# First projections in quarters of the features, small loads moved, and a buffer of its own for the third projection's weights

## The reference, cut to what matters

```
mod = silu(c) @ w_ada + b_ada             # 6 x 1024 columns; c_ctx for the context tile
sh1, sc1, g1, sh2, sc2, g2 = split(mod, 6)
h = layer_norm(x) * (1 + sc1) + sh1
q_a, k_a, v_a, q_g, k_g, v_g, r_g, lr, mg = split(h @ w_in)
attn = attention(rms(q_a), rms(k_a), v_a)        # rotary on latents, cached keys and values
gla  = gated linear attention(q_g, k_g, v_g, decay from lr)  # chunks of 64, both directions
merged = sigmoid(mg0) * (attn @ w_br_attn) + sigmoid(mg1) * (gla * silu(r_g) @ w_br_gla)
x  = layer_norm(alpha * x + g1 * (merged @ w_out))
h2 = layer_norm(x) * (1 + sc2) + sh2
x  = layer_norm(alpha * x + g2 * mixture_of_experts(h2))     # 32 experts, top 1 of 4 groups, top 2 of 8
```

## Time and profile before

| | |
|---|---|
| three executions, us | 663.35, 665.12, 667.0 (median 665.12) |
| the profiled execution, us | 667.03, span 665.3 |
| PE busy | 619.1 us, 93% of the span, 3423 matmul instructions |
| DVE, ACT, POOL busy | 266.9, 107.2, 114.5 us |
| DMA | 176.5 MB, 265 GB/s in the mean |
| longest links of the chain that ended last | PE 70%, DMA 15%, DVE 8% of the span |

### The profile page before, as it was taken

The page is one execution under the profiler, slowest core; times in us unless marked ns, Lnnn a source line. Parts: engine busy times, 40 slices in busy tenths (PEclk is TensorE's granted clock), DMA queues, the critical chain, the costliest instruction groups (busy, mean ns, idle before and its releaser), DMA issues.

```text
span 665.3 us, 8643 instructions
## 1 busy us (share of the span) xinstructions
PE 619.1 (93%) x3423; PEld 348.1 (52%) x3423; DVE 266.9 (40%) x600; ACT 107.2 (16%) x223; POOL 114.5 (17%) x113
## 2 busy tenths in 40 slices
PE   6998999999999999999999999999999987778894
PEld 3553345546455556565554575665565543444541
DVE  4321543135534543302325866334333333222247
ACT  2001543211022322240000012111111111111000
POOL 4000000110300000000001222434334333221101
PEclk9999999999999999999999999999999999999898
DMA  9997737345030330308995089999999999999952
GB/s 340 391 330 282 253 128 254 127 132 186 24 128 9 118 109 19 96 32 244 398 404 249 32 320 355 349 418 415 412 417 417 414 415 413 416 417 418 411 226 95
DMA packets 56120, 176.50 MB, mean 265 GB/s; under 512 B 10378, under 2 KB 12458, under 8 KB 44432
## 3 DMA queue, kind: packets, MB, share of 16 engines
q1 hardware_dynamic: 39264, 143.34, 55.5%
q10 hardware_dynamic: 11152, 24.47, 10.5%
q0 software_dynamic: 5664, 8.14, 3.5%
HBM read 174.32 MB, written 11.96 MB: 280 GB/s over the span
## 4 chain that ended last, share of the span: by engine, by line
PE 70%; DMA 15%; DVE 8%; issue 3%; ACT 2%; POOL 1%; SPq 0%; ACTq 0%; DVEq 0%; POOLq 0%
PE bank L1619 13%; PE bank L1901 12%; PE bank L1608 7%; PE bank L1793 6%; PE bank L1910 5%; DMA Y<-exp_w_up 4%; PE bank L1807 4%; DMA X<-exp_w_up 4%; DMA W<-exp_w_up 4%; PE bank L1572 3%; PE bank L1532 2%; DMA Y<-w_ada 2%; PE bank L1875 2%; POOL rstd L706 1%; PE bank L1760 1%
## 5 line engine op out<-in xcount | busy, mean ns | idle before, releaser
L1901 PE MATMUL bank<-X,Y 128*64 128x256 f32 x672 | 80.6, 389 | 12.4 <-DMA X<-exp_w_up 11.4
L1619 PE MATMUL bank<-Y,W 128*128 128x384 f32 x256 | 86.6, 492 | 0.0
L1901 PEld LDWEIGHTS bank<-X,Y 128*64 128x64 f32 x672 | 51.0, 135 | 46.8 <-DMA X<-exp_w_up 18.4
L706 POOL TENSOR_TENSOR rstd<-ss,cst 128x1 f32<-128x1 f32 (+3 forms) x21 | 22.6, 1074 | 294.4 <-DVE ss L839 294.4
L1619 PEld LDWEIGHTS bank<-Y,W 128*128 128x128 f32 x256 | 47.4, 190 | 36.0 <-issue 5.6
L1608 PE MATMUL bank<-W,Y 128*128 128x512 f32 x144 | 64.0, 598 | 0.0
L749 POOL DMA_INDIRECT Y<-h_rows,gidx x31 | 40.3, 1301 | 86.0 <-PE bank L1875 80.5
L1218 DVE COPY abias<-bank 128x128 f32<-128x128 f32 x32 | 9.3, 292 | 111.5 <-PE bank L1937 111.5
L1901 PE MATMUL bank<-W,Y 128*64 128x256 f32 (+1 forms) x320 | 37.7, 340 | 7.1 <-DMA W<-exp_w_up 3.4
L754 POOL DMA_INDIRECT pair_rows<-PTr,sidx x32 | 32.9, 1029 | 64.6 <-DVE PTr L1232 64.0
L1608 PEld LDWEIGHTS bank<-W,Y 128*128 128x128 f32 x144 | 26.7, 190 | 30.9 <-issue 30.6
(11 more groups left out here) (237 smaller groups left out, 731.5 us busy)
## 6 DMA issues: line engine op xcount, KB each, us to landing
X<-exp_w_gate SPq DMA_DIRECT2D x22, 1024.0 KB, 25.5
X<-exp_w_up SPq DMA_DIRECT2D x22, 1024.0 KB, 26.3
X<-exp_w_down SPq DMA_DIRECT2D x22, 1024.0 KB
Y<-w_ada ACTq DMA_DIRECT2D x16, 1024.0 KB, 8.3
W<-w_in SPq DMA_DIRECT2D x7, 2048.0 KB, 9.2
W<-exp_w_gate SPq DMA_DIRECT2D x10, 1024.0 KB
W<-exp_w_up SPq DMA_DIRECT2D x5, 1024.0 KB
W<-exp_w_down SPq DMA_DIRECT2D x5, 1024.0 KB
```

The source lines that it names most:

```text
L706: nc.gpsimd.tensor_tensor(rstd[:, 0:n], ss[:, 0:n], const("mhalf", 0, n), ALU.pow)\
L1619: ins = mm(bank[:, 0:TOKENS], w[:, k, c * P:(c + 1) * P], hT[:, :, k, :], start=k == 0, stop=k == KT - 1)
L1901: ins = mm(bank[hh * 64:hh * 64 + 64, a:b], x_[:, c, h * 64:h * 64 + 64], rhs(hh), start=k == 0 and a == 0, stop=k == KT - 1, skip_group_c ...
```

## The change

- `w_ada`'s first 2048 columns and the first two projections' weights are loaded in four quarters: quarter g holds columns 256g to 256g+255 of the shift and of the scale (1 MB each) and feature blocks 2g and 2g+1 of `kvl` and `gqk`. PE's `shift_scale(g)` multiplies a quarter of both at once (16 matmuls of 256 columns where `modulation` had 8 of 512), `columns(g)`, `modulate(g)` and `project_quarter(kind, i, g)` follow by quarters.
- Only `ident` and `selcol` are loaded first; the other constants after the second quarter. The small parameters come ahead of the fourth quarter; the router's weights come last, with a semaphore of their own.
- `vg`'s weights go to three pieces of memory that are free until later (`vg_parts`), so their load waits only for `shift_scale(0)`; `q`, `rg` and the rest use the two halves of `W`.
- DVE takes the statistics of tiles 0 and 1 ahead of the silu, and has a slot for each tile's mean and power. The constant -1/2 is set by POOL.
- `keep_busy` is 4 at the start, 1 after the first `columns`; its moving operand is the identity, repeated.
- `ada` entries stand at 3, 6, 7, 8, 9, 10, 11, 13, `rows` 0 at 9 in place of 8. ACT issues eight bias rows in place of four at the start, and the three halves of the ring after `shift_scale(3)`.

The core of the diff:

```diff
-for _n, _j in zip(range(4, 12), (2, 4, 6, 7, 8, 10, 11, 13)):
+for _n, _j in zip(range(4, 12), (3, 6, 7, 8, 9, 10, 11, 13)):
     AFTER[_j].insert(0, ("ada", _n))
-AFTER[8].insert(0, ("rows", 0))
+AFTER[9].insert(0, ("rows", 0))
...
-FILL_START = 6
+FILL_START = 4
+FILL_QUARTER = 1
...
+QUARTERED = ("kvl", "gqk")
+QUARTERS = 4
+QK = KT // QUARTERS
+QD = QK * P
...
+        vg_parts = [(qT.rearrange("p i k t -> p (i k t)"), 0, 3), (Pr.rearrange("p b n -> p (b n)"), 3, 6),
+                    (q.rearrange("p i n -> p (i n)"), 6, 8)]
...
-            sp.dma_start(cst[:, :], T["consts"][:, 0:NCONST]).then_inc(S["consts_in"], 16)
+            early_consts = CAT["incl_f"]
+            sp.dma_start(cst[:, 0:early_consts], T["consts"][:, 0:early_consts]).then_inc(S["first_consts_in"], 16)
...
+            def load_shift_scale(g):
+                h = slice(QD * (g % 2), QD * (g % 2 + 1))
+                for n in (g // 2, 2 + g // 2):
+                    sp.dma_start(early[n][:, g % 2], wa[:, :, n * HALF + h.start:n * HALF + h.stop])\
+                        .then_inc(shift_scale_in[g], 16)
...
+            for g in range(QUARTERS):
+                load_shift_scale(g)
+                load_quarter(g)
+                if g == 1:
+                    sp.dma_start(cst[:, early_consts:], T["consts"][:, early_consts:NCONST]).then_inc(S["consts_in"], 16)
+                if g == 2:
+                    small_loads()
+            main.wait_full(sp, "shift_scale", 0)
+            for a, k0, k1 in vg_parts:
+                sp.dma_start(a[:, 0:(k1 - k0) * HALF].rearrange("p (k n) -> p k n", n=HALF),
+                             wi[:, k0:k1, OFF[5]:OFF[5] + HALF]).then_inc(S["vg_in"], 16)
+            router_weights()
...
+            first_norm_stats(0)
+            first_norm_stats(1)
+            first_norm(0)
+            silu_of_cond()
+            first_norm_stats(2)
+            first_norm(1)
+            first_norm(2)
+            for g in range(QUARTERS):
+                shift_scale(g)
+                modulate(g)
...
-            for n in range(4):
-                bias_rows(n)
+            for g in range(QUARTERS):
+                quarter_bias_rows(g)
...
-            main.wait_full(act, "ada", 3)
+            main.wait_full(act, "shift_scale", QUARTERS - 1)
             for h in range(3):
                 ada_half(h)
...
+            def shift_scale(g):
+
+                pe.wait_ge(shift_scale_in[g], 32)
+                bank = main.claim(pe, "shift_scale", g)
+                for s in range(2):
+                    w = early[2 * s + g // 2][:, g % 2]
+                    for k in range(KT):
+                        j = k % 4
+                        ins = mm(bank[32 * j:32 * j + 32, s * QD:(s + 1) * QD], csil[:, k, :], w[:, k, :], start=k < 4,
+                                 stop=k >= 4, skip_group_check=True)
+                main.filled(ins, "shift_scale", g)
...
             keep_busy(FILL_START)
             x_transposes(0)
             x_transposes(1)
             pe.wait_ge(S["cond_silu"], 2)
-            modulation(0)
+            shift_scale(0)
             x_transposes(2)
...
+            columns(0)
+            keep_busy(FILL_QUARTER)
+            for g in range(QUARTERS - 1):
+                for i in range(TILES):
+                    project_quarter("kvl", i, g)
+                project_quarter("gqk", 0, g)
+                shift_scale(g + 1)
+                project_quarter("gqk", 1, g)
+                columns(g + 1)
+                project_quarter("gqk", 2, g)
```

More of the change, by code:

```diff
@@ L97, in constants @@
     put("unused", np.repeat(EMPTY + (rows // SLOT_ROWS)[:, None], 2 * NE, 1))
-    put("mhalf", np.full((P, 8), -0.5))
     c[:, NCONST:] = 2 * np.arange(TOKENS)[None] + (rows // SLOT_ROWS)[:, None]
     return c
-WEIGHTS = ([("ada", 0)]
-           + [(x, 0) for x in ("kvl", "gqk", "vg", "q", "rg")] + [("mg", n) for n in range(4)]
+WEIGHTS = ([(x, 0) for x in ("kvl", "gqk", "vg", "q", "rg")] + [("mg", n) for n in range(4)]
            + [("br", n) for n in range(2)])
@@ L199, in wait_read @@
         eng.wait_ge(self.at[job][2], self.at[job][3] + 1)
-HALVED = ("kvl", "gqk")
+QUARTERED = ("kvl", "gqk")
+QUARTERS = 4
+QK = KT // QUARTERS
+QD = QK * P
 def first_jobs():
-    jobs = {("modc", g): 7 for g in range(2)}
+    jobs = {("modc", g): 7 for g in range(QUARTERS)}
     jobs.update({("xT", 0, 0): 0, ("xT", 0, 1): 1, ("xT", 1, 0): 3, ("xT", 1, 1): 0, ("xT", 2, 0): 1, ("xT", 2, 1): 3})
-    jobs.update({("ada", n): 2 for n in (0, 2, 1, 3, 4)})
-    for kind, ring in zip(HALVED, ((4, 5, 6), (3, 0, 1))):
+    jobs.update({("shift_scale", g): 2 for g in range(QUARTERS)})
+    jobs[("ada", 4)] = 2
+    for kind, ring in zip(QUARTERED, ((4, 5, 6), (3, 0, 1))):
         jobs.update({("proj", kind, 0, i): ring[i] for i in range(TILES)})
@@ L239, in main_jobs @@
     for j, x in enumerate(PROJ):
-        jobs += [("proj",) + x for _ in range(x[0] not in HALVED)] + [step for step in AFTER[j] if step[0] == "ada" and step[1] > 4]
+        jobs += [("proj",) + x for _ in range(x[0] not in QUARTERED)] + [step for step in AFTER[j] if step[0] == "ada" and step[1] > 4]
     jobs += [("br", c, m) for c in range(KT) for m in range(2)]
@@ L593, in _ @@
+            router_weights()
+            for j, (kind, n) in enumerate(ring):
                 buf = W[:, j % 2, :]
@@ L631, in _ @@
             load_gate_up(sp, 1, 1, ew_in[1])
[L632 to L633 removed]
+            sp.wait_ge(w_free[(len(ring) - 1) % 2], (len(ring) + 1) // 2)
+            sp.wait_ge(w_free[len(ring) % 2], len(ring) // 2)
             load_gate_up(sp, 3, 3, ew_in[3])
@@ L843, in power @@
                 dve.wait_ge(S["pow_done"], powers[0])
-            def norm(src, dst):
-                for g in range(2):
-                    step(V.bn_stats(stats[:, g, :], src[:, g * HALF:(g + 1) * HALF]))
-                step(V.bn_aggr(mv[:, :], stats[:, 0:2, :].rearrange("p a b -> p (a b)")))
-                power(ss[:, 0:1], mv[:, 1:2], 1.0, EPS)
-                return V.tensor_scalar(dst, src, mv[:, 0:1], rstd[:, 0:1], ALU.subtract, ALU.mult)
             def half_stats(src, g):
@@ L1313, in _, with quarter_bias_rows @@
             act.wait_ge(S["zeros_set"], 5)
+            def quarter_bias_rows(g):
+                bias, landed = quarter_bias(g)
+                for s in range(2):
+                    act.dma_start(bias[0:2, s * QD:(s + 1) * QD],
+                                  T["b_ada"][0:1, s * D + g * QD:s * D + (g + 1) * QD].to_broadcast([2, QD]))\
+                        .then_inc(landed, 16)
             def bias_rows(n):
@@ L1534, in modulation, with shift_scale, columns @@
                 main.filled(ins, "ada", n)
[L1535 to L1545 removed]
+            def shift_scale(g):
+                pe.wait_ge(shift_scale_in[g], 32)
+                bank = main.claim(pe, "shift_scale", g)
+                for s in range(2):
+                    w = early[2 * s + g // 2][:, g % 2]
[4 more added lines that the diff above has]
+                main.filled(ins, "shift_scale", g)
+            def columns(g):
+                bank = side.claim(pe, "modc", g)
+                main.wait_read(pe, "shift_scale", g)
+                for s in range(2):
+                    for j in range(QK):
+                        at = 2 * (s * KT + QK * g + j)
+                        c = s * QD + j * P
+                        ins = mm(bank[:, at:at + 2], part[:, g, c:c + P], const("selcol"), start=True, stop=True)
+                side.filled(ins, "modc", g)
             def keep_busy(count):
                 for _ in range(count):
[L1550 removed]
+                    mm(banks[6][:, :], ident, ident.unsqueeze(1).to_broadcast([P, HALF // P, P]), start=True, stop=True)
             def x_transposes(i):
```

241 lines of the change are left out of this document (102 added, 139 removed).

## The result

The kernel after the change takes **667.65 us** (median of 20 runs, 664.68 to 669.86), the kernel before 665.48 us (median of 20 runs beside them, 662.54 to 667.26). The ratio is 1.0035, 95% interval 1.0023 to 1.0048: slower by 1.5 to 3.2 us. I had forecast 663.3, a gain of 1.8. The time lies in my range, but the kernel is slower where I had forecast a gain; on that side I had given rival C (PE's clock) 0.15 and rival B (a late `ada` 4) 0.15. Ratios and mean clocks leave out executions more than 1.5% above the fastest of their kernel, of which there is one here, of e8 (671.05 us).

A forecast was written before the change was run, and what follows sets the result against it. PE's work was taken to bound the kernel, with gains only ahead of 25.26 us; `cum` 0 3.7 sooner less one `ada` (1.9) still to come nets 1.8, so 665.12 - 1.8 = 663.3 us, range 659.5 to 668.0.

The forecast's parts named there:

- rival C: PE's clock falls to its lower level in gaps of 1.9 and 3.8 us, 3.1 us each: 666.4 or 669.5; chance 0.15.
- rival B: `ada` 4's second ring half, issued only after `shift_scale(3)`, lands up to 2.9 us late, delaying the chain: 666.2; chance 0.15.
- The end of `ada` 4: On PE, after the fourth `kvl` quarter and `gqk` of tile 0, `ada` 4 ends at S + 33.3 + 6.7 = 59.2.
- S: Start of PE's first projection: 19.2 us, bounds 18.0 to 20.5, with second transposes at 13.1 set by DVE's order.
- `shift_scale`'s price: One quarter's shift and scale on PE, 32 instructions of 256 columns for 16 of 512: 1.95 us.
- Rival D: `shift_scale` is bound by its instructions, 3.5 us instead of 1.95, four times: 6.2 more, 669.5; chance 0.08.
- The quarters: First stage on PE: 11.1 us a quarter (`kvl`, `gqk`, `shift_scale`, 0.85 more), 33.3 for three.
- The moved small loads cost nothing, covered by this lead: Some 14 issues on SP ahead of the fourth quarter, which still lands before 44 and is needed at 46: no cost.
- The chain to the second `z`: Behind `ada` 4, DVE's bias add and key norm 4.3, gate step 4.2, with hand-overs 8.7: second `z` at 67.9.
- rival A: PE does not stand in the key norm's chain, so 3.8 us are not lost: 659.5; chance 0.20.
- From there to `cum` 0: From the second `z` to `cum` 0 on PE 12.5 us as before, so `cum` 0 starts at 80.4.
- The 1.27 us wait "stays": PE's 1.27 us wait for `w_ada` at 96.13 remains, as ACT issues that half at the same point of the order.

The follow-up runs named there:

- e8: e7 with DVE's last subtraction of each gate step moved behind the next key norm; 663.07 us, ratio 0.9960 to the kernel before.
- e9: Kernel after plus two PE fills between the transposes of tiles 0 and 1 only; 667.30 us, ratio 1.0030 to the kernel before.
- e13: Kernel after plus fills between the transposes of tiles 0 and 1, between `ada` 4's halves and ahead of the second `z`; 665.35 us, ratio 1.0004.
- e2: Kernel after plus two fills between the transposes of tiles 0 and 1 and three ahead of the second `z`; 665.44 us, ratio 1.0011.
- e1: Kernel after run again with no edit, as base of the others; 667.75 us, ratio 1.0039 to the kernel before.
- e3: Kernel after with the first key norm put ahead of `ada` 4's bias add, on DVE alone; 666.97 us, ratio 1.0019 to the kernel before.
- e7: Kernel after with e9's fill, e5's load order, gate work started earlier in the table and side banks changed; 667.81 us, ratio 1.0038.
- e15: Repeat of the best version: e8 with one ring half issued a quarter earlier, after `shift_scale(2)`; 660.25 us, ratio 0.9917 to the kernel before.
- e14: e15 without the split of DVE's gate step; 667.50 us, ratio 1.0027 to the kernel before.
- e4: Kernel after with the three ring halves issued by ACT after `shift_scale` 1, 2 and 3 instead of all after 3; 674.63 us, ratio 1.0144.
- e5: Kernel after with the 14 small loads issued behind the fourth quarter instead of ahead of it; 667.02 us, ratio 1.0017 to the kernel before.
- e6: Kernel after with the edits of e2 and e5 together; 665.88 us, ratio 0.9998 to the kernel before.

## Why the prediction was wrong, point by point

Two terms of the sum failed. The end of `ada` 4, put at 59.2, came at 61.5 to 61.9, and with it the second `z`, which bounds all that follows. And the clock behind PE's gaps has no term in the sum, only a rival's place; the runs show 2.0 to 2.4 us for it.

- **S, the first projection's start**: forecast 19.2, with the clock kept 19.21 (e9) and 18.88 (e13). The number was hit in part by luck: I let DVE's order set it, with the second transposes at 13.1 and the first quarter landed by 13.2; in e13 the transposes start at 12.29, and PE then waits 0.52 us for the quarter, which is there at 13.90. In the kernel after it is 20.08, because the first `shift_scale` runs at the lower level (3.01 for 1.93 us).
- **`shift_scale`'s price**: forecast 1.95, measured 1.93 for 32 records of 256 columns beside 1.92 for 16 of 512. Rival D fell.
- **The quarters**: 11.1 us forecast, 11.0 measured (24.87 to 35.89).
- **"The moved small loads cost nothing, covered by this lead"** failed in part. I let the fourth quarter land before 44; it comes at 46.0, 0.9 before PE asks, since SP spent 8 us on the small issues. Where the clock is kept and PE comes earlier, it waits 0.5 (e13), 1.75 (e9) or 1.91 us (e2). I had counted "up to 10 us of SP's queue" and not subtracted it from the lead.
- **`ada` 4**: rival B's mechanism with a smaller size. ACT issued its halves at 48.90 (forecast 48.1, formerly 39.51); PE waited 0.90 us, 1.32 in e1. The forecast ended `ada` 4 at 59.2; it ends at 61.5 in the profile after, at 61.9 in e1 and at 61.8 in e13. In e1 1.1 of the 2.7 us came before its start (0.85 from S) and 1.5 are its late second half. There is a second link that I missed, `lr` 0 and the bank out of which `ada` 4's result must first be read (1.07 us); it made the chain behind no longer than forecast.
- **The chain to the second `z`**: "with hand-overs 8.7" behind the end of `ada` 4; measured 8.8 (61.5 to 70.27). The length was right, my reason only half: e3 took the key norm out of it and won next to nothing, as a second path is as long: bank, `lr` 0, `z` 0; behind both come the gate step and the eviction of `lr` 1. So rival A fell too: PE does stand in this chain. With its late start the second `z` came at 70.27 instead of 67.9, and this alone makes `cum` 0 2.4 us later than forecast.
- **The 1.27 us wait "stays"**: wrong in my favour. It is gone after the change and 0.5 us in e13.
- **The clock, rival C, decided.** Both of its gaps are there, 2.17 us for 1.9 and 2.64 for 3.8, and both are followed by the lower level. I priced a fall at 3.1 us, which is twice too much for this profile, and doubted it because the expert stage keeps 0.99 in spite of 20.7 us of waits. In the profile after the first costs 1.1 us in `shift_scale` and 0.3 in the transposes ahead of it, the second 0.4 in `z` and 1.2 in `vg` of tile 0, and more in e1 (`vg` 9.5 us instead of 7.03). By medians the whole of rival C is 667.75 - 665.35 = 2.4 us (e1 to e13).

The sum put right, by e1's profile: the second `z` is 2.8 us late (70.66 for 67.9). From there to `cum` 0 it is 15.7 us and not 12.5, as `z` and `vg` of tile 0 run at the lower level: 3.2 more. Behind `cum` 0 1.9 come back (40.0 us to `intra` 0 where the forecast needs 41.9), 1.3 of them the `w_ada` wait that is gone. Together -1.8 + 2.8 + 3.2 - 1.9 = +2.3, the measured loss. In e13 the same sum without a fall is -1.8 + 2.9 - 0.1 - 1.2 = -0.2; its median is indeed about that of before (ratio 1.0004). So of the 4.1 us between my forecast (-1.8) and the result (ratio 1.0035, +2.3), about 1.6 to 2.1 are the late start of the chain and 2.0 to 2.4 the clock. The parting isn't exact: e13's fill between the halves of `ada` 4 ends at 60.7 and may itself delay the chain by some tenths.

The Trainium skill (TensorE: Matmul & The Clock Gate, section HAM oscillation — how this bites in real kernels) says that a TensorE which waits for its data is throttled to half its clock and starts its next piece of work cold, and that work should be arranged so that it stays warm. This case agrees as to the mechanism: 0.50 granted behind both gaps. Fills that feed nothing, which e13 uses to the same end, brought it back to 1.00 there.

What stays open: why the second fall is short in one execution (`intra` 0 at 124.31) and long in another (126.40); what makes the clock fall in e7 and not in e8 behind nearly the same waits; what the fill ahead of the second `z` is worth by itself (it was only run beside the first); and how much of e8's lead over e7, and of e15's over e14, a fill alone would have given, which wasn't tried (for e7 the estimate above says little).

## What to carry to other kernels

A gap in front of the bounding engine has two prices, its length and the slower clock of the work behind it; where a change concentrates short waits in one place, reckon with both, and try a fill in each gap before judging the order. When steps are reordered, follow the PSUM banks and the in-order evictions as well as the engines: here a result waiting for one engine's read held up another chain through a shared bank, and a step that waits for ACT in the middle of DVE's order cost more than the whole change was to bring. A lead of loads is a sum over the issuing queue too: here fourteen small issues ahead of a large one took 8 us of lead.

## What the hardware showed that I had not expected

- The granted clock fell to 0.50 behind the first gap where it was 2.17 us (after, e1, e3, e4) and not where it was 2.11 (e5). It fell behind the gap ahead of the second `z`, 2.33 to 2.65 us, in all six profiles of the old table that have it without a fill (after, e1, e3, e4, e5, e9). In the kernel before, with waits of 0.2 to 1.3 us in this stage, it did not fall.
- It also fell at 62 to 65 us behind two shorter waits close together: 0.96 and 1.07 us (e9), 1.28 and 0.96 (e3), 1.48 and 0.75 (e7), 1.77 and 1.07 (e6), 1.88 and 1.07 (e5). In e1 (1.32 and 1.07), e2 (0.93 and 1.07) and e8 (1.59 and 0.75) it did not. So in these profiles the length of a wait alone does not tell whether the clock falls.
- Halving a matmul's columns from 512 to 256 with four column strips of 32 side by side cost nothing (1.93 against 1.92 us for the same sum).
- The first transfer, 65 KB, landed 2.0 us after its issue, so the fills began at 2.85 and not at 3.4 us (at 3.32 and 3.40 in e13 and e9); 700 KB had taken 4.2.
